# A decoder layer on one core: the depthwise convolution of the last two fronts moves from TensorE to VectorE, and the pooling weights are loaded once

## The reference

```python
proj = h @ w_in                      # pool values | z | x,B,C | dt | two gates
a = pool_mixer(pool_in, pool_w, pool_scale)          # 4 groups, windows 2/4/8/16, a 256x256 map for each group
xbc = silu(causal_depthwise_conv(xbc, conv_w, conv_b))   # 4 taps, 4,096 channels
y = ssd_scan(xs, dt, a, bmat, cmat)                  # Mamba-2 chunked scan
h = layer_norm(alpha*h + (sigmoid(g_pool)*a + sigmoid(g_ssm)*m) @ w_out)
# PEER: for each token 8 heads x 16 experts out of 16,384
hdot = einsum('td,thkd->thk', h, expert_u[idx])
out  = einsum('thk,thkd->td', gelu(hdot)*gate, expert_v[idx])
h = layer_norm(alpha*h + out)
```

## Time and profile before

| | us |
|---|---|
| median of 3 runs | 3649.55 (3647.32 to 3651.27) |
| the profiled execution | 3651.32 |
| its span, first to last instruction | 3649.6 |
| PE, PEld, DVE, ACT, POOL busy | 2878.3, 2053.1, 2678.8, 1066.4, 2069.4 |
| mean granted TensorE clock | 0.858 of full speed |
| moved by DMA | 1389.7 MB, 381 GB/s on average |

### The profile page before, as it was taken

The page is one execution under the profiler, slowest core; times in us unless marked ns, Lnnn a source line. Parts: engine busy times, 40 slices in busy tenths (PEclk is TensorE's granted clock), DMA queues, the critical chain, the costliest instruction groups (busy, mean ns, idle before and its releaser), DMA issues.

```text
span 3649.6 us, 46261 instructions
## 1 busy us (share of the span) xinstructions
PE 2878.3 (79%) x16076; PEld 2053.1 (56%) x16076; DVE 2678.8 (73%) x5760; ACT 1066.4 (29%) x2756; POOL 2069.4 (57%) x1839
## 2 busy tenths in 40 slices
PE   8986989789889879999988779999977853443443
PEld 7886887677777427777775437787754410000000
DVE  3418756899975888777776887777776886668667
ACT  5522632244322214444313114444212110001000
POOL 0003433576655667766666676667766676555552
PEclk9998999899899879999999879999988866555555
DMA  6557999999999999999999999999999999999997
GB/s 247 204 229 305 379 373 384 367 376 398 380 343 360 410 409 398 400 409 402 400 410 411 410 399 385 407 403 393 410 383 411 402 400 415 421 421 422 421 421 312
DMA packets 315415, 1389.71 MB, mean 381 GB/s; under 512 B 35504, under 2 KB 41008, under 8 KB 250672
## 3 DMA queue, kind: packets, MB, share of 16 engines
q0 software_dynamic: 262656, 1073.86, 73.9%
q1 hardware_dynamic: 51232, 308.18, 21.3%
q10 hardware_dynamic: 1296, 4.72, 0.3%
HBM read 1382.43 MB, written 4.19 MB: 380 GB/s over the span
## 4 chain that ended last, share of the span: by engine, by line
DMA 25%; PE 25%; POOL 12%; issue 5%; DVE 4%; ACT 1%; DVEq 0%; POOLq 0%; ACTq 0%
POOL rowbuf L607 10%; PE main L650 10%; DMA rowbuf<-ev,idx 8%; DMA rowbuf<-euv,idx 5%; PE vbank L738 4%; DMA ring<-euv,idx 3%; PE main L658 3%; PE main L869 2%; PE main L854 2%; DMA merged<-euv,idx 2%; DVE acc L1738 2%; DMA xT<-euv,idx 2%; PE turn L721 2%; DMA rowbuf<-eu,idx 1%; DMA late<-euv,idx 1%
## 5 line engine op out<-in xcount | busy, mean ns | idle before, releaser
L607 POOL DMA_INDIRECT rowbuf<-eu,idx x722 | 847.2, 1173 | 801.3 <-DVE hdot L1712 280.4
L607 POOL DMA_INDIRECT rowbuf<-ev,idx x717 | 774.5, 1080 | 397.7 <-issue 191.8
L1712 DVE CUSTOM_DVE_ANT_0 rowbuf<-rowbuf,hb 128x1024 f32<-128x1024 f32 x637 | 778.8, 1224 | 162.9 <-DMA rowbuf<-eu,idx 96.0
L650 PE MATMUL main<-xT,ring 128*128 128x256 f32 (+1 forms) x4480 | 804.7, 340 | 13.5 <-DMA ring<-wblocks 10.8
L650 PEld LDWEIGHTS main<-xT,ring 128*128 128x128 f32 x4480 | 720.2, 193 | 99.0 <-issue 29.7
L738 PE MATMUL vbank<-rowbuf,vdiag 64*64 64x512 f32 x2992 | 494.4, 758 | 260.9 <-DMA rowbuf<-ev,idx 138.9
L1738 DVE SCALAR_TENSOR_TENSOR acc<-rowbuf,hact,acc 128x1024 f32<-128x1024 f32 x427 | 549.8, 1288 | 89.6 <-DMA rowbuf<-ev,idx 80.3
L738 PEld LDWEIGHTS vbank<-rowbuf,vdiag 64*64 64x64 f32 x2992 | 104.2, 156 | 572.4 <-ACT vdiag L1090 318.2
L1090 ACT ACTIVATE vdiag<-spots,hact 128x64 f32<-128x64 f32 x531 | 167.9, 344 | 549.3 <-DVE hact L1721 343.9
L854 PE MATMUL main<-late,ring 128*128 128x256 f32 (+1 forms) x1280 | 237.0, 349 | 32.2 <-issue 21.2
L854 PEld LDWEIGHTS main<-late,ring 128*128 128x128 f32 x1280 | 211.2, 199 | 57.3 <-issue 25.1
(11 more groups left out here) (251 smaller groups left out, 3845.3 us busy)
## 6 DMA issues: line engine op xcount, KB each, us to landing
ring<-wblocks SPq DMA_DIRECT2D x280, 1024.0 KB, 8.1
rowbuf<-eu,idx POOLq DMA_INDIRECT x722, 12.8
rowbuf<-ev,idx POOLq DMA_INDIRECT x717, 12.6
pw<-poolw SPq DMA_DIRECT2D x20, 256.0 KB, 9.5
h_out<-acc ACTq DMA_DIRECT2D x8, 512.0 KB
xT<-xt SPq DMA_DIRECT2D x3, 1024.0 KB, 13.4
zy<-x SPq DMA_DIRECT2D x3, 1024.0 KB, 13.7
rowbuf<-euv,idx POOLq DMA_INDIRECT x84, 20.0
```

The lines of the kernel that those rows point to most:

```text
L607: pool.indirect_dma_start(rows[r], None, (eu, ev)[table], bass.IndirectOffsetOnAxis(ap=idx[c % 2][:, u, k:k + 1], axis=0)).then_inc(row_re ...
L650: last = pe.matmul(dst_[:, ct * tc:(ct + 1) * tc], w[:, k, ct * P:(ct + 1) * P], src[:, k, 0:tc], start=(k == 0), stop=(k == KD - 1))
L1712: last = dve.tensor_tensor_reduce(r, r, h, 1.0, 0.0, ALU.mult, ALU.add, hdot[:, g % 2, k:k + 1])
```

## The change

The convolution of fronts 3 and 4 takes the form of fronts 0 to 2. `FILL`, `conv_weights`, `convolve`, the semaphore `conv_raw` and the tile `cdiag` go. The result banks `turn` then have 32 turns fewer. The pooling on VectorE is spread over places 4 to 8 in all fronts but the first. `pw` holds all four maps, loaded in front 0 only, each with its own semaphore. Some tiles move without a change of work: `cbs` gets a tile of its own, `tmi` and `pos` lie in unused columns of `merged`, and `mask`, used at the start only, in `vdiag`. The number of row buffers and the tables `WIDTHS` and `SHARES` stay.

```diff
-FILL = 3
@@ made_turn
-        return not (c < FILL and m % TA in CONV or CHUNK[c] < NT and m % TA in (6, 9))
+        return not (m % TA in CONV or CHUNK[c] < NT and m % TA in (6, 9))
@@ tiles
-        pw = sb("pw", [P, 2, 256])
+        pw = sb("pw", [P, AJ, 2, 256])
-        cdiag = sb("cdiag", [P, 2, TAPS, P])
-        cbs = cdiag[:, 0, :, :]
+        cbs = sb("cbs", [P, 2 * NT, P])
@@ SyncE, superchunk(c)
-                    if j:
-                        sp.wait_ge(turn_ready, turns(c, (j - 1) * TA + 3) + TURNED)
-                    elif c:
-                        sp.wait_ge(turn_ready, turns(c - 1, 3 * TA + 3) + TURNED)
-                    sp.dma_start(pw[:, :, :], poolw[ds(j, 1), :, :, :].rearrange("o p k n -> (o p) k n")
-                                 ).then_inc(pw_ready, 16)
+                    if c == 0:
+                        sp.dma_start(pw[:, j, :, :], poolw[ds(j, 1), :, :, :].rearrange("o p k n -> (o p) k n")
+                                     ).then_inc(pw_ready[j], 16)
@@ TensorE
-            def convolve(c, j, n):
-
-                pe.wait_ge(conv_raw, (c - FILL) * 4 * AJ + j * 4 + n + 1)
-                dst_ = turn_bank(c, j * TA, CONV[n])
-                tc = CHUNK[c] * P
-                for ct in range(2):
-                    for k in range(TAPS):
-                        last = pe.matmul(dst_[:, ct * tc:(ct + 1) * tc], cdiag[:, ct, k, :], craw[:, n % 2, ct, k:k + tc],
-                                         start=(k == 0), stop=(k == TAPS - 1))
-                last.then_inc(turn_ready, 1)
@@ front_a1
-                    if n >= 3 and c >= FILL:
-                        convolve(c, j, n - 3)
@@ front_a2
-                if c >= FILL:
-                    unturned(pe, c, j * TA + 2)
-                else:
-                    pe.wait_ge(conv_out, (c * AJ + j) * 4 + 2)
+                pe.wait_ge(conv_out, (c * AJ + j) * 4 + 2)
@@ ScalarE, raw_conv
-                if c < FILL:
-                    for ct in range(2):
-                        last = act.activation(conv_tile(n)[:, ct, 0:tc], src[:, ct, :], ACT.Copy,
-                                              scale=cw[:, ds(j * 8 + n * 2 + ct, 1), TAPS - 1:TAPS].rearrange("p a b -> p (a b)"))
+                for ct in range(2):
+                    last = act.activation(conv_tile(n)[:, ct, 0:tc], src[:, ct, :], ACT.Copy,
+                                          scale=cw[:, ds(j * 8 + n * 2 + ct, 1), TAPS - 1:TAPS].rearrange("p a b -> p (a b)"))
@@ VectorE, the loop over column groups
-                        weave(o(8 if c < FILL else 12), pooling(c, j, False), 4)
-                        if c < FILL:
-                            for n in range(4):
-                                weave(o((9, 12, 15, 18)[n]), convolution(c, j, n), 1)
+                        weave(o(8), pooling(c, j, False), 4)
+                        for n in range(4):
+                            weave(o((9, 12, 15, 18)[n]), convolution(c, j, n), 1)
```

54 lines of the change are left out of this document (15 added, 39 removed).

## The result

**Slightly slower.** After: 3662.02 us, median of 22 runs (3648.18 to 3672.48). Before, run beside it: 3651.39 (3644.64 to 3659.15). The ratio is 1.0026, 95% interval 1.0017 to 1.0036. The forecast was 3636.5 and faster. The profiled execution took 3657.05 us with a span of 3655.2, against 3651.32 and 3649.6; between these two lie 5.7 us, between the medians 10.6. The windows of the eight groups that change, and the first of the next stage, answer to rows 3.

A forecast was written before the change was run, and what follows sets the result against it. The prediction took TensorE as the bound in fronts 3 and 4, DMA a close second. The slower of VectorE and DMA per group gave 812.7 us against 830.4, -17.7; giving back 5 left -13: median 3636.5 us, range 3622 to 3665.

The forecast's parts named there:

- the slower case: Fronts 3 and 4, first 19 places: VectorE becomes the bound and keeps its waits; +18 us, 3668; chance 0.24.
- the likeliest case: Eight groups of fronts 3 and 4 get faster, median 3636.5 us, own range 3623 to 3642; chance 0.54.
- So TensorE sets the pace and DMA is a close second.: In the eight groups TensorE, 94 to 98% busy, is the bound; DMA share is 0.98 to 1.02 at 386 to 409 GB/s.
- DMA's need: Each group's bytes less 0.26 MB, at 411 GB/s: 97.1 to 105.4 us a group.
- Each group lasts as long as the slower of VectorE and DMA: The eight groups' sum: 812.7 us against 830.4 today, -17.7 us before 5 us are given back.
- The 11.5 us of GpSimd for TensorE ... come from TensorE being late, and that goes.: In group 2, GpSimd's 11.5 us wait for TensorE to free row buffers goes once TensorE loses its convolution.
- GpSimd's need: Some 62 gathers a group at 1.15 us, with 0.30 between two: 90 us, under the other engines.
- VectorE's price: The convolution costs VectorE 2.70 us a block, four blocks a group: 10.8 us a group in fronts 3 and 4.
- point of decision: VectorE's idle time in a group: at 10.7 us the length is kept; if 13 remain, each group is 2.3 us longer.
- The pooling weights: 16 of 20 loads go, 8 in fronts 3 and 4 at 0.65 us each: 5.2 us in all where DMA bounds.
- The clock: TensorE's clock may fall to 0.90 to 0.92 as in front 2; 84 us become 93, groups end no later.
- The rule against it: Gathers held by VectorE's blocks cost GpSimd up to 10.8 us a group, 3650 to 3660 us; chance 3 in 100.

The follow-up runs named there:

- Run 7: Kernel before, with three of four taps of TensorE's convolution left out in fronts 3 and 4, nothing added on VectorE: 3662.02 us, ratio 1.0023.
- run 14: Changed kernel; in fronts 3 and 4 TensorE takes 0.3 of first-part v rows and 0.6 in place of 0.8 in the second part: 3668.75 us, 1.0037.
- run 17: Changed kernel, with the second z projection moved from the scan to ahead of the B/C transposes in fronts 3 and 4 only: 3637.91 us, 0.9971.
- Run 5: Changed kernel, with two of four taps left out in fronts 3 and 4, so VectorE makes two multiply-adds a block, not six: 3654.91 us, 1.0008.
- run 2: Kernel before, with pooling weights loaded in front 0 only, later fronts using its last group's map: 3649.22 us, 0.9991.
- run 10: Changed kernel, with 20 idle matmuls a group in a free bank where TensorE waits for B and C in fronts 3 and 4: 3663.68 us, 1.0023.
- 8: Kernel before, three of four TensorE taps left out in fronts 3 and 4, 24 idle matmuls ahead of projection 6 of each group: 3657.08 us, 1.0018.
- run 6: Changed kernel, with 32 idle matmuls a group on TensorE ahead of projections 4 to 6 in fronts 3 and 4: 3653.61 us, 1.0009.

## Why the prediction was wrong

The measured 3662.02 us lies inside the forecast's wide range of 3622 to 3665, but only because that range reached into the slower case, which had a chance of 0.24; the mechanism and the sign of the likeliest case were wrong.

**The step that failed: "So TensorE sets the pace and DMA is a close second."** It was read from a busy share of 94 to 98%. Run 7 takes three quarters of the convolution off TensorE and nothing gets faster. In the sum, where TensorE had already been set aside, the term that failed is DMA's need "at the best rate of a stage with rows and weight blocks, 411 to 412 GB/s". The eight groups moved 332.2 MB, which at 411 are 808 us; they moved them at 396 and took 839.1. In the first part TensorE was busy 58.70 of 58.70 us, and DMA was full at the same time, at 403 GB/s. In nineteen of the twenty profiles of this study the first parts ran at 402 to 407 GB/s (399 in run 14), whoever made the convolution and however long they were: their length is bytes by rate. A shorter TensorE only pulled weight blocks forward into them: in run 7 6.9 of the 7.5 MB more are direct loads. The forecast had a DMA bound in it, but by whole groups: "Each group lasts as long as the slower of VectorE and DMA". A group has two parts with different limits, and the traffic that the second part fails to carry can't be made up in the first, which is full. Of the second parts' rate (341 to 404 GB/s over the runs) the forecast said nothing, and it is what the runs differ in.

**"The 11.5 us of GpSimd for TensorE ... come from TensorE being late, and that goes."** It does not. The wait is behind one projection of 7 us that the hand-written order puts into the scan. Run 7 leaves it at 67.0 us of 69.5; run 17 takes the projection out of the scan and leaves 14.9. In the changed kernel it fell to 37.7 while the wait for VectorE rose from 41.0 to 75.4; as run 7 shows no such fall, I put it down to VectorE's lateness, which no run shows alone.

**GpSimd's need, "90 us, which is under the others",** missed that its waits and issues come on top. In front 3 its gathers are 245 in number and busy 285.9 us, the issue gaps 66.5 and the waits for VectorE and TensorE 53.9: together 406 of 405.4 us. GpSimd was never idle for another reason, and any wait added there lengthens the group. After the change it is 288.5, 66.5 and 57.5 us of 412.1. The convolution raised the wait for VectorE from 17.4 to 36.2 us, but the one for TensorE fell by 15.2, so the waits explain 3.6 of the 6.7 us; the other 3.1 are gathers that took longer.

**VectorE's price was right; the slower rival was right in sign and wrong in place.** A block takes 2.79 us, where rows 7 have 2.78 for a block and 2.70 up to the next start. VectorE's busy time rose by 9.3 us a group, not 10.8. The rival said "The place is the first 19 places of a group". They did grow by 30.3 us, but by moved bytes, at an unchanged rate. Its point of decision (10.7 us idle left to VectorE) does not order the groups: those of front 3 keep 8.9, 16.1, 14.4 and 9.7 us idle and changed by +4.5, +0.8, +2.5 and -1.1 us against rows 3: of the two below 10.7 us one lost most and the other gained. On average, though, it holds: 13.3 us of idle time were left in a group, just the 13 that it named for +18. That price was too high (the groups show +8.7, the medians +10.6), because busy time grew by less than its 10.8. Run 5 gives 6 to 7 us back by taking two thirds of VectorE's added work away, run 7 loses the whole without any. The two effects overlap and do not add.

**The pooling weights** were taken as 0 to 5 us: run 2 gives 2.4 us with an interval that holds zero. **The pooling's place** cost nothing, as said. **The clock** fell as in front 2 (0.88 to 0.95). In the first parts that cost nothing that can be measured (run 10), as said; in the second parts no run raised it alone. **The rule against it** did not show. Beside blocks of the convolution GpSimd's gathers read:

```profile
1510.64 1.00 POOL L602 DMA_INDIRECT rowbuf<-ev,idx  x1 [0.30 <-issue]
1511.95 1.05 POOL L602 DMA_INDIRECT rowbuf<-eu,idx  x1 [0.30 <-issue]
1513.31 1.04 POOL L602 DMA_INDIRECT rowbuf<-ev,idx  x1 [0.30 <-issue]
1514.95 1.73 POOL L602 DMA_INDIRECT rowbuf<-eu,idx  x1 [0.60 <-DVE hdot L1662]
1516.99 1.05 POOL L602 DMA_INDIRECT rowbuf<-ev,idx  x1 [0.30 <-issue]
1520.00 1.74 POOL L602 DMA_INDIRECT rowbuf<-eu,idx  x1 [1.96 <-DVE hdot L1662]
```

VectorE's blocks ran from 1510.75 to 1513.54 and from 1515.80 to 1518.59. Over the whole of front 3, 28 gathers ran beside a block for more than 0.3 us and took 1.03 us on average, the others 1.20; the 19 that lay wholly inside a block took at most 1.06. The mean of all is 1.18 against 1.17 before. The Trainium skill (SBUF — State Buffer, SBUF: two separate sides) says that a VectorE instruction with two inputs in SBUF takes the shared port pair for its whole length against a GpSimd instruction that reads SBUF; no such hold shows on the gathers of this trace. What does reach GpSimd is the dot product behind the block: 0.60 and 1.96 us of waiting.

**What stays open.** That less work on TensorE buys nothing is shown (7), and that the loss is a lower rate in the second parts is seen in 7, 8 and the changed kernel alike. Why the second parts are worse when TensorE's projections come earlier is not settled. A lower clock alone does not explain it (run 17 has 401 GB/s at 0.82 to 0.94, run 6 386 at 0.96 to 1.00 in seven of eight), though a part of the loss may be its doing; nor do fewer direct loads in the second part (8). The stop of group 0 points to fewer gathers under way when GpSimd stops; that is not tested. A hold of the blocks within a group, which would test the draws themselves, was not tried, and whether the move of run 17 would help the kernel before, where TensorE never waits ahead of those transposes in fronts 3 and 4, was not tried either.

## What to carry to other kernels

A busy share near 100% is no proof of a bound: before costing a relief, take some of that engine's work away alone (run 7 was an edit of two lines) and see whether anything moves. For a wait behind an engine, read in order of time which instruction stands in front of what is waited for; a single 7 us block in the wrong place outlives any relief elsewhere. And where a move opens a wait on one engine, look for the work on the same engine that is on the chain later: moved into the hole, it turned +0.26% into -0.29%, but only in the fronts that had the hole.

## What the runs showed of the hardware

- Gathers alone can fill the DMA engines. In run 17 the second parts have almost no direct loads (0.8 MB in 297.2 us), and 118.3 MB of rows went through, 398 GB/s on average. The 345 GB/s of the changed kernel's second part in group 0 is therefore not a limit of gathering.
- Idle matmuls raised the granted clock in the first parts, from between 0.88 and 0.93 to between 0.95 and 1.00, and the kernel's time did not change (1.0023 against 1.0026, run 10).
- A full DMA share of 1.01 stood beside 395 as well as 403 GB/s in the changed kernel's groups; the share alone doesn't tell a lossless window from a lossy one.
- Gathers issued inside VectorE's convolution blocks took at most 1.06 us, less than the mean of 1.18 (the changed kernel, front 3).
